# Latent attention heads: value product with high and low values in one stationary tile of 128 columns, two matmuls a step instead of three, and the one low feature that does not fit summed by VectorE

## The reference, cut to what matters

```python
def mla_attention(q, k, v):
    ...
    def block(args):
        qb, qch = args
        s = jnp.einsum('bqhd,bkhd->bhqk', qb, k).astype(jnp.float32) * scale
        mask = key_chunk[None, :] <= qch[:, None]
        s = jnp.where(mask[None, None], s, NEG)
        p = jax.nn.softmax(s, axis=-1)
        return jnp.einsum('bhqk,bkhd->bqhd', p.astype(v.dtype), v)
```

## Time and profile before

| | |
|---|---|
| median of 3 runs | 2159.89 us (2156.31 to 2160.33) |
| the profiled execution | 2159.98 us, span 2158.2 us, 1.8 us around it |
| TensorE busy | 2107.0 us, 98% |
| VectorE, ScalarE, GpSimd busy | 1434.8, 1041.5, 1090.5 us |
| attention stage with diagonal and off-diagonal steps | from 450.9 to about 891 us |
| its blocks u = 2 and 3 | from 604.5 us on |

### The profile page before, as it was taken

How to read it: one execution, slowest core, us unless ns; L and a number is a source line. 1 busy time by engine, 2 the same in 40 slices (tenths; PEclk the granted TensorE clock), 3 DMA queues, 4 the chain that set the end, 5 groups by cost and what they waited for, 6 DMA issues and landing times. The chain is left out here.

```text
span 2158.2 us, 30875 instructions
## 1 busy us (share of the span) xinstructions
PE 2107.0 (98%) x9992; PEld 1744.9 (81%) x9992; DVE 1434.8 (66%) x2110; ACT 1041.5 (48%) x1870; POOL 1090.5 (51%) x892
## 2 busy tenths in 40 slices
PE   8999999899999999989999999999999999999999
PEld 6899999777777777768888878888888888888887
DVE  5688888977666656578767787766635644354463
ACT  6566666567777667644333443333423233222221
POOL 2566666644575757567656676556346710020220
PEclk9999999999999999999999999999999999999999
DMA  7133233688675756755444754444677752234363
GB/s 244 45 106 100 84 112 119 207 241 251 196 237 178 221 182 193 253 187 173 160 161 142 246 177 157 143 141 159 223 240 272 244 204 98 98 137 136 132 224 113
DMA packets 293440, 374.20 MB, mean 173 GB/s; under 512 B 27149, under 2 KB 187117, under 8 KB 291518
## 3 DMA queue, kind: packets, MB, share of 16 engines
q1 hardware_dynamic: 293310, 372.56, 53.3%
HBM read 247.28 MB, written 125.19 MB: 173 GB/s over the span
## 5 line engine op out<-in xcount | busy, mean ns | idle before, releaser
L128 PE MATMUL bank<-f_t_hi,f_w_hi 128*128 128x512 f32 x896 | 351.0, 392 | 12.2 <-DVE f_w_lo L1888 7.1
L128 PE MATMUL bank<-f_t_lo,f_w_hi 128*128 128x512 f32 x896 | 350.3, 391 | 0.0
L128 PE MATMUL bank<-f_t_hi,f_w_lo 128*128 128x512 f32 x896 | 350.1, 391 | 0.0
L128 PE MATMUL bank<-f_w_hi,f_a_hi 128*128 128x512 f32 x896 | 348.5, 389 | 0.0
L128 PE MATMUL bank<-f_w_lo,f_a_hi 128*128 128x512 f32 x896 | 348.5, 389 | 0.0
L128 PE MATMUL bank<-f_w_hi,f_a_lo 128*128 128x512 f32 x896 | 348.5, 389 | 0.0
L2739 POOL TENSOR_TENSOR a_p_lo<-a_prob,a_p_hi 128x512 fp32r<-128x512 f32 (+1 forms) x192 | 234.2, 1231 | 164.8 <-DVE a_p_hi L2888 67.4
L128 PEld LDWEIGHTS bank<-f_t_hi,f_w_hi 128*128 128x128 f32 x896 | 169.2, 189 | 50.3 <-issue 14.1
L2039 POOL TENSOR_TENSOR f_r<-f_r,f_y 128x512 f32<-128x512 f32 x24 | 42.0, 1788 | 325.0 <-DMA f_r<-s_x 325.0
L2140 DVE TENSOR_TENSOR f_a_lo<-f_a_raw,f_a_hi 128x1024 fp32r<-128x1024 f32 x112 | 158.5, 1415 | 71.6 <-ACT f_a_hi L2064 71.4
L128 PEld LDWEIGHTS bank<-f_t_hi,f_w_lo 128*128 128x128 f32 x896 | 169.2, 189 | 35.5
(11 more groups left out here) (347 smaller groups left out, 4833.7 us busy)
## 6 DMA issues: line engine op xcount, KB each, us to landing
f_a_raw<-s_aop SPq DMA_DIRECT2D x112, 512.0 KB, 4.4
w_raw<-in_w_ff SPq DMA_DIRECT2D x64, 512.0 KB, 5.3
s_aop<-f_a SPq DMA_DIRECT2D x128, 256.0 KB, 4.4
s_aop<-f_s SPq DMA_DIRECT2D x96, 256.0 KB, 2.4
f_w_raw<-in_w_ff SPq DMA_DIRECT2D x64, 256.0 KB, 5.9
f_t_raw<-s_hop SPq DMA_DIRECT2D x14, 1024.0 KB, 8.1
f_r<-in_w_ff SPq DMA_DIRECT2D x48, 256.0 KB, 6.3
a_vals<-s_v SPq DMA_DIRECT2D x40, 264.0 KB, 4.9
```

What stands on the lines that cost most here:

```text
L128: ins = pe.matmul(out, a, b, start=(first and j == 0), stop=(last and j == n - 1))
```

## The change

The stored value rows are laid out anew. The high row keeps 64 features and has one column of ones; the low row's feature 1 follows directly, so that columns 0 to 127 of the flattened tile are: 64 high features, one, low features 1 to 63. Column 128 is low feature 0, columns 129 to 131 are zero. `value_lows` writes this with two GpSimd instructions instead of one.

A latent step then has a matmul of all 128 columns by `p_hi` and one of all 128 by `p_lo`. PSUM row 64+i gathers the low part of feature i. For low feature 0, in steps with `summed_low` (off the diagonal, u = 2 or 3: 80 steps) VectorE adds `p_hi` times the value column into `low_sum`, and at the unit's last step one matmul sums `low_sum` over the partitions into row 0. In the other 80 latent steps a third matmul with a stationary tile of 2 columns does it. After `stage`, `merge` adds rows 65 to 127 to `mixed`. Memory steps stay as they were. The ring of `p_lo` falls from 5 buffers to 4, whose fifth holds `low_sum`.

```diff
                 def value_lows(t):
...
-                    pool.tensor_tensor(lv[:, :, 1, 0:LV], lkv[:, :, LN:], lv[:, :, 0, 0:LV].bitcast(F32), ALU.subtract).then_inc(lv_lo_done, 1)
+                    flat = lv[:, :, :, :].rearrange("p h e d -> p h (e d)")
+                    pool.tensor_tensor(flat[:, :, LV + 1:2 * LV], lkv[:, :, LN + 1:], flat[:, :, 1:LV].bitcast(F32), ALU.subtract)
+                    pool.tensor_tensor(flat[:, :, 2 * LV:2 * LV + 1], lkv[:, :, LN:LN + 1], flat[:, :, 0:1].bitcast(F32), ALU.subtract).then_inc(lv_lo_done, 1)
...
-    R32, RP, RS = 4, 5, 2
+    R32, RP, RP4, RS = 4, 5, 4, 2
...
+    summed_low = [on_act[s] and units[x[0]]["u"] >= 2 for s, x in enumerate(steps)]
+    low_before = [sum(summed_low[:s]) for s in range(N + 1)]
+    for r in range(N):
+        if summed_low[r]:
+            put("sum_low", r + 3, r)
+    for U, x in enumerate(units):
+        if x["hd"]["causal"]:
+            put("merge", end_of(U) + LAG + (0 if U + 1 == NUNITS else 1), U)
...
+    def reads_done(eng, s):
+
+        if s >= 0:
+            wait(eng, low_done, low_before[s + 1])
...
                 sp.wait_ge(pv_done, piece_last[n - VR] + 1)
+                reads_done(sp, piece_last[n - VR])
...
-                wait(pool, pv_done, s + 1 - RP)
+                wait(pool, pv_done, s + 1 - RP4)
...
                     wait(ac, pv_done, s + 1 - RP)
+                    reads_done(ac, s - RP)
...
+        def sum_low(r):
+            U, k, c0, d0 = steps[r]
+            n, low = piece_at(U, k), low_of(U)
+            first = vals[:, n % VR, k % (CW // P), 1, VD - 2:VD - 1].bitcast(F32)
+            hi_wait(dve, r)
...
+            if r == low[0]:
...
+                dve.tensor_scalar(low_sum[:, :], p_hi[r % RP][:, :].bitcast(F32), first, None, ALU.mult).then_inc(low_done, 1)
+            else:
+                dve.wait_ge(low_done, low_before[r])
+                dve.scalar_tensor_tensor(low_sum[:, :], p_hi[r % RP][:, :].bitcast(F32), first, low_sum[:, :].bitcast(F32), ALU.mult, ALU.add
+                                         ).then_inc(low_done, 1)
+
+        def merge(U):
+            tile, half = units[U]["hd"]["out"]
+            part = mixed[units[U]["u"] % 2][half * VD:(half + 1) * VD, tile, :]
+            dve.wait_ge(staged, U + 1)
...
+            dve.scalar_tensor_tensor(part, pO[U % 2][VD:2 * VD, :], low_mask[VD:2 * VD, 0:1], part, ALU.mult, ALU.add).then_inc(merged, 1)
...
             dve.wait_ge(spread, 2 * g + i + 1)
+            dve.wait_ge(merged, 2 * g + 2)
...
             for r in of("cast", s):
                 cast(r)
+            for r in of("sum_low", s):
+                sum_low(r)
...
                 dve.reciprocal(inv[:, part], srow[:, part]).then_inc(inverted, 1)
+            for U in of("merge", s):
+                merge(U)
...
-                products(pe, pO[U % 2][0:VW, c0:], [(vt[:, 0, :], vt[:, 1, :], p_hi[r % RP][:, c0:], p_lo[r % RP][:, c0:])],
-                         first=(k == 0), last=(r + 1 == end_of(U))).then_inc(pv_done, 1)
+                high, low = p_hi[r % RP][:, c0:], p_lo[r % RP4][:, c0:]
+                if not units[U]["hd"]["causal"]:
...
+                else:
+                    vt = vt.rearrange("p e d -> p (e d)")
+                    if k == 0:
+                        wait(pe, merged, U // 2)
+                    pe.matmul(pO[U % 2][:, c0:], vt[:, 0:P], high, start=(k == 0), stop=False)
+                    if not summed_low[r]:
+                        pe.matmul(pO[U % 2][0:2, c0:], vt[:, P:P + 2], high, start=False, stop=False)
+                    if r + 1 == end_of(U) and low_of(U):
+                        pe.wait_ge(low_consts, 4)
+                        pe.wait_ge(low_done, low_before[r])
+                        pe.matmul(pO[U % 2][0:2, :], low_pick[:, :], low_sum[:, :], start=False, stop=False)
+                    pe.matmul(pO[U % 2][:, c0:], vt[:, 0:P], low, start=False, stop=(r + 1 == end_of(U))).then_inc(pv_done, 1)
...
                 if g == LAST:
+                    if i:
+                        pe.wait_ge(merged, NUNITS // 2)
```

More of the change, by code:

```diff
@@ L844, in _ @@
                 pool.memset(prob[:, :, KEYS:], 0.0).then_inc(const_made, 1)
-                for e in range(2):
-                    wait(pool, const_made, 9 + e)
-                    pool.memset(lv[:, :, e, LV:].bitcast(F32), 1.0 - e).then_inc(const_made, 1)
+                wait(pool, const_made, 9)
+                pool.memset(lv[:, :, 0, LV:LV + 1].bitcast(F32), 1.0).then_inc(const_made, 1)
+                wait(pool, const_made, 10)
+                pool.memset(lv[:, :, 1, LV - 1:].bitcast(F32), 0.0).then_inc(const_made, 1)
                 pool.wait_ge(const_made, 11)
@@ L2510, in attend_and_project, with low_of @@
     act_before = [sum(on_act[:s]) for s in range(N + 1)]
+    summed_low = [on_act[s] and units[x[0]]["u"] >= 2 for s, x in enumerate(steps)]
[6 more added lines that the diff above has]
+            put("merge", end_of(U) + LAG + (0 if U + 1 == NUNITS else 1), U)
+    def low_of(U):
+        return [r for r in range(units[U]["start"], end_of(U)) if summed_low[r]]
+    def reads_done(eng, s):
+        if s >= 0:
+            wait(eng, low_done, low_before[s + 1])
     def count_to(name, slot):
@@ L2531, in attend_and_project @@
     p_hi = [sb(f"p_hi{b}", [P, UQ], F32R, at=last_rows + 2 * KB * b) for b in range(RP)]
-    p_lo = [sb(f"p_lo{b}", [P, UQ], F32R, at=last_rows + 2 * KB * (RP + b) if b < 3 else first_rows + 2 * KB * (3 + b)) for b in range(RP)]
+    p_lo = [sb(f"p_lo{b}", [P, UQ], F32R, at=last_rows + 2 * KB * (RP + b) if b < 3 else first_rows + 2 * KB * (3 + b)) for b in range(RP4)]
+    low_sum = sb("low_sum", [P, UQ], F32R, at=first_rows + 14 * KB)
     room["at"] = E["end"] - F["base"]
@@ L2541, in attend_and_project @@
     zeros = sb("zeros", [P, P])
+    low_pick, low_mask = sb("low_pick", [P, 2], F32R), sb("low_mask", [P, 1])
     assert room["at"] <= 80 * KB
@@ L2570, in attend_and_project @@
     staged, inverted, spread, scaled = sem("staged"), sem("inverted"), sem("spread"), sem("scaled")
+    low_done, merged, low_consts = sem("low_done"), sem("merged"), sem("low_consts")
     row_hi_done, row_lo_done, picks_made = sem("row_hi_done"), sem("row_lo_done"), sem("picks_made")
@@ L2731, in gpsimd @@
         pool.wait_ge(const_made, 10)
+        pool.memset(low_mask[:, :], 1.0).then_inc(low_consts, 1)
+        pool.wait_ge(low_consts, 1)
+        pool.memset(low_mask[VD:VD + 1, :], 0.0).then_inc(low_consts, 1)
+        pool.wait_ge(low_consts, 2)
+        pool.memset(low_pick[:, 0:1].bitcast(F32), 1.0).then_inc(low_consts, 1)
+        pool.wait_ge(low_consts, 3)
+        pool.memset(low_pick[:, 1:2].bitcast(F32), 0.0).then_inc(low_consts, 1)
         pool.tensor_scalar(pick_r[:, :, :], pick[:, :, :], 1.0, 1.0, ALU.mult, ALU.mult).then_inc(picks_made, 1)
@@ L2737, in gpsimd @@
                 hi_wait(pool, s)
-                wait(pool, pv_done, s + 1 - RP)
-                pool.tensor_tensor(p_lo[s % RP][:, c0:], prob[s % R32][:, c0:], p_hi[s % RP][:, c0:].bitcast(F32),
+                wait(pool, pv_done, s + 1 - RP4)
+                pool.tensor_tensor(p_lo[s % RP4][:, c0:], prob[s % R32][:, c0:], p_hi[s % RP][:, c0:].bitcast(F32),
                                    ALU.subtract).then_inc(lo_done, 1)
@@ L2887, in cast @@
             wait(dve, pv_done, r + 1 - RP)
+            reads_done(dve, r - RP)
             dve.tensor_copy(p_hi[r % RP][:, c0:], prob[r % R32][:, c0:]).then_inc(hi_dve, 1)
+        def sum_low(r):
[3 more added lines that the diff above has]
+            hi_wait(dve, r)
+            if r == piece_first[n] or r == low[0]:
+                dve.wait_ge(v_loaded[n % VR], 16 * (n // VR + 1))
+            if r == low[0]:
+                if low_before[r]:
+                    dve.wait_ge(pv_done, end_of(U - 2))
+                dve.tensor_scalar(low_sum[:, :], p_hi[r % RP][:, :].bitcast(F32), first, None, ALU.mult).then_inc(low_done, 1)
[7 more added lines that the diff above has]
+            dve.wait_ge(staged, U + 1)
+            if U == 1:
+                dve.wait_ge(low_consts, 2)
+            dve.scalar_tensor_tensor(part, pO[U % 2][VD:2 * VD, :], low_mask[VD:2 * VD, 0:1], part, ALU.mult, ALU.add).then_inc(merged, 1)
         def scale(g, i):
@@ L3020, in tensor @@
                 vt = vals[:, n % VR, k % (CW // P), :, :]
-                products(pe, pO[U % 2][0:VW, c0:], [(vt[:, 0, :], vt[:, 1, :], p_hi[r % RP][:, c0:], p_lo[r % RP][:, c0:])],
-                         first=(k == 0), last=(r + 1 == end_of(U))).then_inc(pv_done, 1)
+                high, low = p_hi[r % RP][:, c0:], p_lo[r % RP4][:, c0:]
+                if not units[U]["hd"]["causal"]:
+                    products(pe, pO[U % 2][0:VW, c0:], [(vt[:, 0, :], vt[:, 1, :], high, low)],
+                             first=(k == 0), last=(r + 1 == end_of(U))).then_inc(pv_done, 1)
+                else:
[10 more added lines that the diff above has]
```

(1 more changed line is left out.)

## The result

The changed kernel takes 2199.75 us (median of 5 runs, 2197.89 to 2205.18) against 2157.89 for the kernel before: ratio 1.0193, 95% interval 1.0182 to 1.0204. It is 42 us slower, where 8 us faster was forecast, and lies above the forecast range, which ended at 2169 us. The profiled execution has a span of 2196.8 us against 2158.2.

The account below looks back on a forecast made before the run. TensorE, busy 98%, was taken to set the time, with VectorE and GpSimd as cover in u = 2 and 3. Terms: -16.6 + 6.5 + 1.9 = -8.2 us against 2159.98, so 2152 us; range 2143 to 2169.

Parts of the forecast that it names:

- What goes: TensorE, blocks u = 2 and 3: 80 matmuls of 0.23 us go, 8 come back, net 16.6 us saved.
- Wide tiles at nothing: TensorE's value matmuls: wider stationary tiles cost nothing, starts stay 0.23 us apart at 512 moving columns.
- the ring of 4: GpSimd's `p_lo` buffers cut to 4: cost nothing to 0.3 us a stall, in the tail.
- the front: Before the stage: 16 small additional GpSimd instructions, counted as nothing; some 4 us if uncovered.
- The sum's price: VectorE, u = 2 and 3: each `sum_low` takes 0.90 us, between bounds of 0.69 and 1.19.
- rival B: VectorE becomes the bound in u = 2 and 3, deciding from 1.07 us a sum: slower, 2166 us; chance 0.32.
- mixed value, 1.00: Alternative price of a sum on VectorE: 0.63 x 1.19 + 0.37 x 0.69 = 1.00 us, with GpSimd busy 63%.
- VectorE's load: Unit by unit in u = 2 and 3, VectorE's added time; its busy time from 604.5 us rises by 74 us.
- 3 us of lag: VectorE may fall 3 us behind before anybody waits; what is over it costs TensorE 6.5 us in u = 2, 3.
- The merges at nothing: The 8 merges of u = 0 and 1 on VectorE cost nothing with cover, 5.5 us without.
- wrong altogether: Signs: change before 450 or after 900 us, granted clock below 1.00 in u = 2, 3, or wide-tile spacing other than 0.23.
- The tail: Last 10 us: three sums each lengthen a `p_lo` by 0.31 us, last cast 0.9 us later; about 1.9 us.

Follow-up runs that it names:

- e5: The changed kernel without sums and merges, its 80 summed steps with two matmuls only (low parts left out): 2150.64 us.
- e3: The changed kernel without sums and merges, with three matmuls in every latent step (low parts of features 1 to 63 left out): 2159.53 us.
- e11: The changed kernel with 40 sums instead of 80, the other 40 steps taking the third matmul: 2179.50 us.
- e12: The changed kernel without sums (third matmul in all latent steps), the merge moved behind maxima and casts but ahead of the splits: 2163.01 us.
- e10: The changed kernel without sums (third matmul everywhere), merges reading `mixed` instead of the PSUM bank, TensorE not waiting for them: 2161.65 us.
- e4: The changed kernel with neither sum nor third matmul in the 80 summed steps (low feature 0 left out there), merges kept: 2164.13 us.

## Why the prediction was wrong, point by point

1. **What goes: wrong by its size.** 80 matmuls are fewer, at 0.23 us each, as counted. But "a matmul taken away is worth its distance to the next start" fails: 8.9 us for 18.4 (e5 against e3). Its condition, "if nothing else takes the hole", was put down as met. The small waits in the earlier trace rows were read as slack of the other engines; they only say that nobody was late at TensorE's present pace.
2. **Wide tiles at nothing: right**, as were the ring of 4 and the front. e3 is at 1.0003. GpSimd's additional instruction takes 0.21 us (median), 16 times.
3. **The sum's price: mis-sized by a little.** 0.90 was taken, 1.07 measured (76.9 us / 72), exactly where rival B was said to decide. By the prediction's own sum 1.07 gives no change, so this explains some 8 of the 48 us between forecast and result. The first sum of a unit took 0.75 us (8 in 6.0 us), not 0.50; a merge 0.76, not 0.69. The mean of 0.90 came from splits that stand right behind ScalarE's high parts, perhaps when GpSimd is likelier to be idle (not tried). The prediction's own mixed value, 1.00, was the better one. The page "SBUF — State Buffer" of the Trainium skill, by whose full blocking 1.09 was worked out, came closest; the trace agrees with it in that number, though single meetings at 835 us were cheaper than it says.
4. **VectorE's load: nearly right, what it does: wrong.** This is the step that failed most: the sum took 3 us as what VectorE may fall behind before anybody waits, and so gave 6.5 us (with the tail 8.4) for what cost 35.6. Five of the eight stretches of the earlier trace rows, in the changed kernel:

```profile
625.30:651.40 26.10, 20.69 (x94) 15.37 (x93) 25.54 (x40) 14.74 (x32) 16.30 (x11) 1.00 0.70 210
...
762.60:796.30 33.70, 30.01 (x125) 23.09 (x124) 32.03 (x52) 18.38 (x39) 22.54 (x17) 0.95 0.58 170
806.70:837.10 30.40, 27.79 (x117) 20.75 (x116) 26.16 (x40) 19.72 (x41) 14.88 (x12) 0.94 0.42 131
847.60:888.40 40.80, 33.35 (x142) 24.19 (x140) 38.33 (x56) 23.46 (x48) 26.09 (x21) 0.96 0.45 144
897.70:931.00 33.30, 28.99 (x120) 21.85 (x119) 25.39 (x25) 21.86 (x46) 26.28 (x20) 0.90 0.44 143
```

   VectorE's busy time was forecast at 24.3, 32.2, 27.8, 34.7 and 20.9 us; it is 25.5, 32.0, 26.2, 38.3 and 25.4. Over u = 2 and 3 it rose by 84 us where 74 was forecast. But the stretch is not VectorE's time less 3 us of lag: it is VectorE's time and 0.6 to 4.2 us more in the first four rows, since VectorE's own waits don't vanish (and, in the three with a clock of 0.94 to 0.96, some 1.7 us each is TensorE's clock). The last stretch, "hidden" with room to spare, grew from 29.4 to 33.3 us (a part of that is its clock of 0.90). The 3 us of lag were read from two waits, `chunk_max` and `p_hi`. TensorE's waits for the splits (8.1 us), the scaling (3.4) and the merge (13.4) were left out, and even `chunk_max` cost 9.0. e11 shows how the cost depends on the load.
5. **The merges at nothing: wrong, 12.8 us without sums, 18.2 with them.** "Behind it on VectorE stand only the next slot's works" looked at the wrong side: what stands ahead of it was the cost (e12), with TensorE's bank held (e10). That TensorE waits for the merge was named, and then counted as covered by the same 3 us, which no run bears out. Even the 5.5 us given "without cover" for the 8 merges of u = 0 and 1 were too little: these two blocks grew by 9 us.
6. **The clock: not in the sum.** A clock below 1.00 in u = 2 and 3 was a sign of "wrong altogether", and it came. It fell where TensorE had waited, and is worth some 14 us of the 42, by the estimate above; these are inside points 4, 5 and 7.
7. **The tail: 1.9 us forecast.** TensorE waited 3.25 us for one `p_lo`, until 922 us, at the place that was named; the size was wrong. It is part of the sums' 35.6 us.

Rival B came nearest: VectorE late, and slower, at 2166 us. Its size was wrong with the same 3 us, with the merges and with the full value of the saving. Its signs came in part only: TensorE's waits for `a_part_max`, `p_hi` and `p_lo` make 17 us, not 20 and more, and VectorE is busy above 95% in three of the eight stretches (25.5 of 26.1 us in the first).

In one ledger, from 2159.5 (e3): the saving -8.9, merges +13.5 (e5 to e4), sums +35.6, of them 27.0 VectorE's time and 8.6 what the second input adds: 2199.7 us. Taken in the other order, sums are 31.0 and merges 18.2. The forecast had -18.4, 0 and +10.2 (6.5, the tail's 1.9 and the 8 closing matmuls' 1.8) in the same places.

## What to carry to other kernels

When one engine is at 98% and the others at 60 to 70% in lists of fixed order, take a part of the work away for nothing first (an experiment like e5 costs one edit): it says what a saving is worth before its price is paid, here 48% of the count. Price an added instruction by what stands ahead of it in its slot and who holds a buffer for it, not by its engine's mean load; and try its place: at the head of the slot it makes everything behind it wait for its input, behind the splits it comes late itself. The place between was worth 9 us for 16 instructions here.

## What the runs showed of the hardware

In the changed kernel TensorE's granted clock fell seven times in the stage to its half level (1.2 of 2.4 GHz), each time where TensorE had just been waiting, and stayed there for a while although the engine was at work again. Around 526 us:

```profile
525.80 0.48 PE L3091 MATMUL bank<-a_p_hi,a_vals 128*128 128x512 f32 x1 [3.59 <-DVE a_mixed L2945]
...
526.93 0.63 PE L128 MATMUL bank<-e_w_hi,a_m_hi 128*128 128x512 f32 x1
527.36 0.63 PE L128 MATMUL bank<-e_w_lo,a_m_hi 128*128 128x512 f32 x1
527.79 0.63 PE L128 MATMUL bank<-e_w_hi,a_m_lo 128*128 128x512 f32 x1
```

The matmuls start 0.43 us apart instead of 0.23 and are told as 0.63 long. That is most of why TensorE's busy time did not fall with its 72 matmuls (16.6 us): by the estimate above, the half clock made the others some 14 us longer.

The length of the single wait does not decide it. Stretches right behind a wait of 3.59 us, of 2.98, of 1.39 and of 2.22 (as the earlier trace rows; the clock stands behind POOL's count):

```profile
526.20:529.50 3.30, 3.30 (x10) 2.56 (x9) 1.04 (x2) 0.00 (x0) 0.00 (x0) 0.50 0.19 71
506.90:510.00 3.10, 3.10 (x14) 2.47 (x15) 1.06 (x3) 1.26 (x3) 0.74 (x1) 1.00 0.82 222
775.40:778.70 3.30, 3.30 (x10) 2.52 (x9) 3.30 (x4) 2.00 (x4) 1.81 (x2) 0.50 0.76 285
862.00:866.00 4.00, 3.90 (x16) 2.97 (x17) 4.00 (x5) 2.81 (x6) 1.66 (x2) 1.00 0.54 166
```

The other falls stand beside waits of 2.10, 1.44, 1.41, 1.25 and 3.25 us. What tells them from the waits of 2.98 and 2.22 us is not shown. Where the fall comes, the wait costs more than its length; in e10 and e12, whose longest waits between 451 and 930 us are 1.45 and 1.23 us, the clock stays at 1.00 there.

A matmul with a stationary tile of 2 columns and 512 moving columns starts the next one as late as a tile of 128 does. TensorE in order of time in e3:

```profile
701.60 0.40 PE L3088 MATMUL bank<-a_p_hi,a_vals 128*128 128x512 f32 x1
701.84 0.39 PE L3090 MATMUL bank<-a_p_hi,a_vals 128*2 128x512 f32 x1
702.07 0.39 PE L3095 MATMUL bank<-a_p_lo,a_vals 128*128 128x512 f32 x1
```

0.24 us to the narrow one and 0.23 from it to the next: at 512 moving columns, 2 or 128 stationary columns made no difference.
